# Attention scores from three products of high and low halves, with eight probability buffers, in a fused hybrid decoder block

## The chip, the cores and the metric

One program runs on one core of a Trainium2 chip. The metric is the device time of one execution in microseconds (us); lower is better. Engines are named as in the profile: PE is TensorE (PEld its weight loads), DVE is VectorE, ACT is ScalarE, POOL is GpSimd, SP is SyncE. A name with a q behind it (ACTq, POOLq) is that engine's sequencer, which issues DMAs.

## What is computed

One decoder block over 512 tokens of width 2048, all in float32. The part that the change touches is the sliding-window attention: 16 query heads of 64 dimensions on 2 key/value heads, in blocks of 128 queries that each see 256 keys (the first block only its own 128).

```python
def sliding_window_gqa_sinks(q, k, v, sinks):
    ...
    s = jnp.einsum('bnqhgd,bnkhd->bnhgqk', qb, kb).astype(jnp.float32) / math.sqrt(HEAD_DIM)
    ...
    s = jnp.where(mask[None, :, None, None], s, jnp.finfo(jnp.float32).min)
    p = jax.nn.softmax(jnp.concatenate([s, sink], axis=-1), axis=-1)[..., :-1]
    o = jnp.einsum('bnhgqk,bnkhd->bnqhgd', p.astype(v.dtype), vb)

def reference(x, ...):
    h = rms_norm(x, norm_mix_pre)
    z = h @ w_in                      # q | k | v | u | two gates
    q, k = partial_rope(q, pos), partial_rope(k, pos)
    o_attn = sliding_window_gqa_sinks(q, k, v, sinks)
    o_ssm = s5_mixer(u, ...)          # diagonal complex state space model, GELU, GLU
    mixed = (g_attn * (o_attn @ w_branch[:Q_W]) + g_ssm * (o_ssm @ w_branch[Q_W:])) @ w_out
    x = x + rms_norm(mixed, norm_mix_post)
    a = jax.nn.relu(rms_norm(x, norm_mlp_pre) @ w_up)
    return x + rms_norm((a * a) @ w_down, norm_mlp_post)
```

## The kernel before, in words

**Large products.** Every weight matrix is streamed in 436 units of 128x1024 elements through a ring of four. SP loads a unit (L333), ACT rounds it to the fp32r type as the high half `w_hi` (`hi`, L514), DVE subtracts to get the low half `w_lo` (`lo`, L908), and PE multiplies it with the high and low halves of the activations in three fp32r products, high by high, low by high and high by low (`product`, L1641 to L1643), 24 matmuls a unit. ACT may convert unit n once PE has finished unit n-4 (`unit_done`). PE waits for `lo_ready` at each unit. I call the stretch in which PE works on unit n "slot n"; the program of each engine is written as a loop over n, and n on ACT and DVE runs some slots ahead of PE.

**What else lies in the slots.** Units 0 to 15 give q, 16 to 19 give k and v, 20 to 35 the state space input u, 36 to 99 the gates. Small work is put by hand between the conversions. On DVE at n = 9 to 19, `normed` reads a PSUM bank pair of q and `rope_q` rotates it; at n = 8 to 22 the parameters of the state space model are worked out (`params_at`: `coefficients`, `powers`, `b_bar`, `b_even`, `b_lo`). The coefficients leave through a small round trip: PE turns them, ACT copies them at n = 16 (L620, `rows_ready`), POOL stores them (L366) and loads them back spread over the channels (L371, eight DMAs, `coef_landed`), and DVE's `b_bar` at n = 20 waits for them. ACT stores the resulting weights at n = 23 (L613, 2 MB, `b_stored`), and `load_bw(0)` at n = 26 brings back the first part with eight DMAs issued on ACT's queue (L567), after DVE has cleared the buffer (`clear_bw`, L1154, at n = 24). PE first needs that buffer in slot 37 (`bu`, L1749), a product in four row groups of 32.

**The attention.** It runs in eight groups of eight heads (4 pairs), two groups for each block of 128 queries. In slot 24 + g PE computes the scores of group g, in slot 25 + g ACT and DVE do exponentials and the normalisation, in slot 26 + g PE transposes the probabilities, and in slot 27 + g it multiplies them with v. Each of these is cut in four parts k = 0 to 3, put between the four quarters of a unit on PE:

```python
for b in range(2):
    r = slice(HEAD * b, HEAD * b + HEAD)
    ins = mm(side[:, b, first_key(g):2 * P], Q[r, a % 8, n * P:n * P + P],
             KTOK[r, n * P - P + first_key(g):n * P + P], start=True, stop=True)
ins.then_inc(scores_done, 1)
```

So one part a = 4g + k computes two heads, one on partitions 0 to 63 and one on 64 to 127, plain float32 operands, with 256 columns, or 128 in groups 0 and 1 (`first_key`). I call these 24 long and 8 short parts. The waits around them: PE's scores of part a wait until DVE has read the part before (`scores_read`); DVE's `mask_scores(a)` (L1117) waits for `scores_done` and, since the probability buffer `PB` is used in turn, for the transposes of part a - `NPB` (`trans_done`); PE's transposes (L1709) wait for `probs_ready` and for ACT's copy of the transposes before (L580, `pt_ready`). On DVE a slot is: mask of part 0, `lo` of unit n (and in some slots `normed` of u), mask 1, `maxima`, mask 2, `normalise` of the group before, mask 3, `maxima`. On ACT it is: copy (L580) and four exponentials (L588) for k = 0 and 1, copies for k = 2 and 3, the copy of the output (L595), then `hi` of the next unit.

**POOL** loads constants at the start (L359 to L363: the rotary tables, the identity, the mask and `b_rows`), does the round trip above, then waits for `bl_ready`, builds `rotation(0)` (13 us of small operations) and scales the first weights (`c_by_a`, `b_by_state`). `rotation(0)` is first read by DVE in slot 37.

Of the kernel before, what the change touches and what calls it, by code (L numbers as in the profile page):

```python
# [30 lines left out]
P = 128  # L31
# [61 lines left out]
def build(nc, wstream, xT, x_rows, gains, gain_rows, params, b_rows, b_state, c_pad, consts, cols, out):  # L93
# [26 lines left out]
    U = at("u", [CT, T], 112)  # L120
    Q = at("q", [8, T], 128)
    MH = at("m_hi", [KT, T], 112, F32R)

    NPB = 12
    PB = at("probs", [NPB, 2, 256], 144)
# [4 lines left out]
    KTOK = at("k_t", [T], 176)  # L130
    VTOK = at("v_tok", [TT_N, P], 178.5)
    MASK = at("mask", [2 * P], 181)
    SUM0 = at("square_sum", [4, T], 183)
    BB = at("b_bar", [CT, 2, SSM_S], 191)
    BE = at("b_even", [CT, 2, SSM_S], 195)
    tmp = [at(f"param{k}", [4 * ST if k in (8, 9) else ST], 144 + 0.5 * k) for k in range(11)]
    CT4 = at("coef_rows", [P], 150)
    CW = at("coef_by_channel", [4, NW], 160)
    BC = at("b_parts", [CT, 2, 2, 2, SSM_S], 144, F32R)
    BT = [at(f"b_bar_tmp{k}", [CT, SSM_S], 112 + 2 * k) for k in range(2)]  # L140

# [62 lines left out]
    with ExitStack() as ctx:  # L204
# [3 lines left out]
        def sem(name):  # L208
# [7 lines left out]
        x_first, x_landed = [sem(f"x_first{k}") for k in range(4)], [sem(f"x_landed{s}") for s in range(4)]  # L216
        cols_landed = sem("cols_landed")
        first_raw, first_hi, first_lo = sem("first_raw"), sem("first_hi"), sem("first_lo")
# [6 lines left out]
        rope_done, vt_done, v_ready = (  # L225
            sem("rope_done"), sem("vt_done"), sem("v_ready"))
        angle_ready, trig_ready, bb_ready, b1_ready = (
            sem("angle_ready"), sem("trig_ready"), sem("bb_ready"), sem("b1_ready"))
# [74 lines left out]
        def first_key(g):  # L303

            return P if g < 2 else 0
# [41 lines left out]
        def _(pool):  # L347
# [12 lines left out]
            pool.dma_start(IDENT[:], consts[:, 1024:1152]).then_inc(consts_landed, 16)  # L360
            pool.dma_start(MASK[:], consts[:, 1152:1408]).then_inc(consts_landed, 16)
            for r in range(2):
# [89 lines left out]

            pool.wait_ge(start_ready, 1)
            plink(nc.gpsimd.memset(CBD[:], 0.0))
            load_c(0)
            load_b(0)
            pool.wait_ge(bl_ready, 2)
            rotation(0)
            c_by_a(0)
            b_by_state(0)  # L460
            pool.wait_ge(o_ready, 8)
            for c in range(1, CT):
# [45 lines left out]
        def _(act):  # L508
# [89 lines left out]
            for n in range(8, U_GATE):  # L598
# [12 lines left out]
                if n == 23:  # L611
                    act.wait_ge(bl_ready, 2)
                    act.dma_start(b_dram.rearrange("p c a e r s -> p (c a e r s)"),  # L613
                                  BC[:].rearrange("p c a e r s -> p (c a e r s)").bitcast(F32)).then_inc(b_stored, 16)
                if n == 26:
                    act.wait_ge(b_stored, 16)
                    load_bw(0)
# [271 lines left out]
        def _(v):  # L889
# [186 lines left out]
            def normed(out_, b):  # L1076

                v.wait_ge(unit_done, UNIT_END[b])
                link_to(tt(out_, pair(b), both(RSTD[:]), ALU.mult), bank_read, b + 1)

            SWAP = [r ^ 8 if r < ROT else r for r in range(32)]

            def rope_q(b):
                x = Q[:, 2 * b:2 * b + 2]
                v.wait_ge(consts_landed, 48)
                link(nc.vector.stream_shuffle(KV[:], x, SWAP))
                tt(x, x, both(ROPE[:, 0]), ALU.mult)
                link(tt(KV[:], KV[:], both(ROPE[:, 1]), ALU.mult))
                link_to(tt(x, x, KV[:], ALU.add), rope_done, b + 1)
# [63 lines left out]
            def clear_bw(k):  # L1153
# [30 lines left out]
                         16: ((rotation_start, 0),), 17: ((rotation_start, 1),),  # L1184
                         20: ((b_bar,),), 21: ((b_even,),), 22: ((b_lo, 0), (b_lo, 1)), 24: ((clear_bw, 0),)}
            def low_and_inputs(n):
# [5 lines left out]
            for n in range(8, U_GATE):  # L1192
# [9 lines left out]
                if n in (11, 12, 15, 19):  # L1202
                    rope_q({11: 0, 12: 1, 15: 2, 19: 3}[n])
                if n == 21:
                    normed(KV[:], 4)
                if n == 23:
                    rope_k()
                if n == N_SLOT0 + 2:
                    v.wait_ge(b_stored, 16)
                if n >= N_SLOT0 + 2:  # L1210
# [412 lines left out]
        def _(pe):  # L1623
# [43 lines left out]
            for n in range(8, U_U):  # L1667
# [4 lines left out]
                if n == 13:  # L1672
                    pe.wait_ge(consts_landed, 48)
                    pe.wait_ge(coef_ready, 1)
                    nc.tensor.transpose(side[:, 2, 0:P], AST[:, 0:4].rearrange("p k s -> p (k s)"), IDENT[:]
                                        ).then_inc(coef_turned, 1)


            def attention(slot, k):
# [13 lines left out]
                for g in group_of(slot, N_SLOT0):  # L1693
                    a, n = 4 * g + k, g // 2
                    if a >= 1:
                        pe.wait_ge(scores_read, a)
                    for b in range(2):
                        r = slice(HEAD * b, HEAD * b + HEAD)
                        ins = mm(side[:, b, first_key(g):2 * P], Q[r, a % 8, n * P:n * P + P],  # L1699
                                 KTOK[r, n * P - P + first_key(g):n * P + P], start=True, stop=True)  # L1700
                    ins.then_inc(scores_done, 1)
# [11 lines left out]
            for n in range(U_U, U_GATE):  # L1713
# [3 lines left out]
                if n == N_SLOT0:  # L1717
                    pe.wait_ge(rope_done, 5)
                    pe.wait_ge(v_ready, 1)
# [387 lines left out]
```

## Time and profile before

| | us |
|---|---|
| median of 3 runs | 2497.89 (2497.19 to 2498.23) |
| the profiled execution's own time | 2496.64 |
| its span in the trace | 2494.8 |
| PE busy | 2480.9 (99%) |
| DVE busy | 1278.3 (51%) |
| ACT busy | 683.5 (27%) |
| POOL busy | 175.3 (7%) |

The span is what lies between the first and the last record of the profile; the time of the execution has 1.8 us more. Busy time counts overlapping matmuls once. TensorE's granted clock is 0.999 of full speed. A float32 matmul leaves two records in the trace (the x4 of a part's scores is two matmuls), an fp32r matmul one. All that the change touches runs in the first 290 us.

### The profile page before, as it was taken

What the parts mean: (1) busy time and instruction counts of PE and PEld (TensorE: products, weight loads), DVE (VectorE), ACT (ScalarE), POOL (GpSimd) and SP (SyncE); (2) the same over time, 40 slices, a digit from 0 to 9 for tenths busy, and PEclk for the clock granted to TensorE, in tenths of its full rate; (3) what the DMA queues carried; (4) which work ended last, traced back from release to release, by engine and by line L of the source; (5) the groups of instructions that cost most, each with busy time, mean ns of one, the idle gap of its engine ahead of it and who ended that gap; (6) DMA issues with size and microseconds to landing.
All of it is one profiled execution on the core that took longest, in us unless ns stands there. A gap on an engine that the chain in (4) does not pass through costs nothing.

```text
span 2494.8 us, 30358 instructions
## 1 busy us (share of the span) xinstructions
PE 2480.9 (99%) x11741; PEld 2026.8 (81%) x11741; DVE 1278.3 (51%) x1621; ACT 683.5 (27%) x906; POOL 175.3 (7%) x283
## 2 busy tenths in 40 slices
PE   9999999999999999999999999999999999999998
PEld 7866887877888888888888888888888888888887
DVE  7876688896434432264444444344444344444436
ACT  5146222333422222252122222212222221222223
POOL 1120344430000000000000000000000000000000
PEclk9999999999999999999999999999999999999999
DMA  6431343443334453343332332233332223333242
GB/s 218 113 114 43 109 132 106 131 123 102 126 95 151 143 181 97 110 161 102 102 102 91 104 100 93 84 101 101 99 100 95 92 85 100 101 101 101 92 160 101
DMA packets 83592, 278.22 MB, mean 112 GB/s; under 512 B 17984, under 2 KB 18048, under 8 KB 81472
## 3 DMA queue, kind: packets, MB, share of 16 engines
q1 hardware_dynamic: 64368, 233.34, 28.9%
q0 software_dynamic: 6480, 26.55, 3.3%
q10 hardware_dynamic: 12672, 17.34, 2.0%
q8 instruction: 50, 0.82, 0.1%
q14 instruction: 22, 0.18, 0.0%
HBM read 258.24 MB, written 18.94 MB: 111 GB/s over the span
## 4 chain that ended last, share of the span: by engine, by line
PE 97%; DVE 2%; DMA 1%; ACT 0%; issue 0%; ACTq 0%; POOL 0%; DVEq 0%
PE main L1641 15%; PE main L1643 15%; PE main L1642 15%; PE side L1837 6%; PE side L1836 6%; PE side L1835 6%; PE main L1836 5%; PE main L1837 5%; PE main L1835 5%; PE side L1642 5%; PE side L1641 5%; PE side L1643 5%; PE side L1699 1%; PE side L1709 1%; PE side L1780 1%; PE side L1688 1%
## 5 line engine op out<-in xcount | busy, mean ns | idle before, releaser
L514 ACT ACTIVATE w_hi<-w_raw 128x1024 fp32r<-128x1024 f32 x435 | 452.6, 1056 | 1079.0 <-PE main L1643 403.3
L908 DVE TENSOR_TENSOR w_lo<-w_raw,w_hi 128x1024 fp32r<-128x1024 f32 x435 | 529.1, 1234 | 358.9 <-ACT w_hi L514 340.0
L1641 PE MATMUL main<-h_hi,w_hi 128*128 128x512 f32 x1280 | 505.7, 395 | 1.3 <-DVE h_lo L924 0.7
L1643 PE MATMUL main<-h_hi,w_lo 128*128 128x512 f32 x1280 | 499.2, 390 | 0.0
L1642 PE MATMUL main<-h_lo,w_hi 128*128 128x512 f32 x1280 | 498.9, 390 | 0.0
L1641 PEld LDWEIGHTS main<-h_hi,w_hi 128*128 128x128 f32 x1280 | 240.6, 188 | 56.8 <-issue 4.7
L1643 PEld LDWEIGHTS main<-h_hi,w_lo 128*128 128x128 f32 x1280 | 240.7, 188 | 50.8
L1642 PEld LDWEIGHTS main<-h_lo,w_hi 128*128 128x128 f32 x1280 | 240.9, 188 | 48.0
L1641 PE MATMUL side<-h_hi,w_hi 128*128 128x512 f32 x512 | 199.2, 389 | 0.0
L1642 PE MATMUL side<-h_lo,w_hi 128*128 128x512 f32 x512 | 199.2, 389 | 0.0
L1643 PE MATMUL side<-h_hi,w_lo 128*128 128x512 f32 x512 | 199.2, 389 | 0.0
L1835 PE MATMUL main<-w_hi,a_hi 128*128 128x512 f32 x496 | 192.9, 389 | 0.0
L1836 PE MATMUL main<-w_hi,a_lo 128*128 128x512 f32 x496 | 192.9, 389 | 0.0
L1837 PE MATMUL main<-w_lo,a_hi 128*128 128x512 f32 x496 | 192.9, 389 | 0.0
L1835 PE MATMUL side<-w_hi,a_hi 128*128 128x512 f32 x496 | 192.9, 389 | 0.0
L1836 PE MATMUL side<-w_hi,a_lo 128*128 128x512 f32 x496 | 192.9, 389 | 0.0
L1837 PE MATMUL side<-w_lo,a_hi 128*128 128x512 f32 x496 | 192.9, 389 | 0.0
L1513 DVE TENSOR_TENSOR mlp_acc<-side,mlp_acc 128x1024 f32<-128x1024 f32 x60 | 70.7, 1220 | 151.3 <-PE side L1837 151.3
L1513 DVE TENSOR_TENSOR mlp_acc<-main,mlp_acc 128x1024 f32<-128x1024 f32 x58 | 68.3, 1220 | 151.2 <-PE main L1837 151.2
L834 ACT ACTIVATE a_hi<-a 128x1024 fp32r<-128x1024 f32 x31 | 32.9, 1061 | 377.3 <-DVE a L1498 377.3
L1641 PEld LDWEIGHTS side<-h_hi,w_hi 128*128 128x128 f32 x512 | 96.1, 188 | 20.0
L1643 PEld LDWEIGHTS side<-h_hi,w_lo 128*128 128x128 f32 x512 | 96.1, 188 | 19.9
(332 smaller groups left out, 3131.2 us busy)
## 6 DMA issues: line engine op xcount, KB each, us to landing
w_raw<-wstream SPq DMA_DIRECT2D x435, 512.0 KB, 3.5
gate_scratch<-gate_stage ACTq DMA_DIRECT2D x16, 512.0 KB, 3.9
gate_attn<-gate_scratch POOLq DMA_DIRECT2D x8, 512.0 KB, 3.7
gate_ssm<-gate_scratch POOLq DMA_DIRECT2D x8, 512.0 KB, 4.4
x_rows<-x_rows POOLq DMA_DIRECT2D x4, 1024.0 KB, 11.6
x_scratch<-x_rows ACTq DMA_DIRECT2D x4, 1024.0 KB, 4.0
x_all<-x_scratch POOLq DMA_DIRECT2D x4, 1024.0 KB, 8.1
x<-x_t POOLq DMA_DIRECT2D x6, 512.0 KB, 6.6
```

The lines of the kernel that those rows point to most:

```text
L514: nc.scalar.activation(WH[:, s], RAW[:, s], ACT.Copy).then_inc(hi_ready, 1)
L834: nc.scalar.activation(AH[:, buf, 2 * half:2 * half + 2], AA[:], ACT.Copy).then_inc(ah_ready, 1)
L908: tt(WL[:, s], RAW[:, s], WH[:, s].bitcast(F32), ALU.subtract).then_inc(lo_ready, 1)
L1513: ins = tt(o, ps, o, ALU.add)
L1641: mm(o, wh, xh[:, k0 + k], start=first and k == 0, stop=False)
L1642: mm(o, wh, xl[:, k0 + k], start=False, stop=False)
L1643: ins = mm(o, wl, xh[:, k0 + k], start=False, stop=last and k == 3)
L1688: ins = mm(side[HEAD * b:HEAD * b + HEAD, 3], VTOK[:, n + kb - 1, HEAD * b:HEAD * b + HEAD], PTB[:, b, kb].rearrange("p a q -> p (a q)"), ...
L1699: ins = mm(side[:, b, first_key(g):2 * P], Q[r, a % 8, n * P:n * P + P], KTOK[r, n * P - P + first_key(g):n * P + P], start=True, stop=True)
L1835: mm(banks[:, t], xh[:, k0 + k, r], wh[:, c], start=first and k == 0, stop=False)
L1836: mm(banks[:, t], xl[:, k0 + k, r], wh[:, c], start=False, stop=False)
L1837: ins = mm(banks[:, t], xh[:, k0 + k, r], wl[:, c], start=False, stop=last and k == 1)
```

## The change

It splits q and k after the rotary step into high halves (`QH` in two tiles, `KH`; ACT copies to fp32r) and low halves (`QL`, `KL`; DVE subtractions), and PE forms each part's scores as three fp32r products, high by high, low by high and high by low, accumulated in the same PSUM banks. To make room for these tiles, `NPB` goes from 12 to 8, the `b_rows` input and its products move to where x lay (so that their load waits on POOL for the end of the reading of x), the mask is loaded later, `rotation(0)` waits for the last scores, and `clear_bw(0)` and `load_bw(0)` move from n = 24 and 26 to n = 34 and 35.

```diff
...
     Q = at("q", [8, T], 128)
+    QL = at("q_lo", [8, T], 128, F32R)
+    QH = [at(f"q_hi{k}", [4, T], kib, F32R) for k, kib in enumerate((191, 160))]
+    KH = at("k_hi", [T], 180, F32R)
+    KL = at("k_lo", [T], 176, F32R)
     MH = at("m_hi", [KT, T], 112, F32R)
...
-    NPB = 12
+    NPB = 8
     PB = at("probs", [NPB, 2, 256], 144)
...
     KTOK = at("k_t", [T], 176)
-    VTOK = at("v_tok", [TT_N, P], 178.5)
-    MASK = at("mask", [2 * P], 181)
+    VTOK = at("v_tok", [TT_N, P], 178)
+    MASK = at("mask", [2 * P], 182)
     SUM0 = at("square_sum", [4, T], 183)
-    BB = at("b_bar", [CT, 2, SSM_S], 191)
-    BE = at("b_even", [CT, 2, SSM_S], 195)
+    BB = at("b_bar", [CT, 2, SSM_S], 112)
+    BE = at("b_even", [CT, 2, SSM_S], 116)
...
-    CW = at("coef_by_channel", [4, NW], 160)
+    CW = at("coef_by_channel", [4, NW], 176)
...
-    BT = [at(f"b_bar_tmp{k}", [CT, SSM_S], 112 + 2 * k) for k in range(2)]
+    BT = [at(f"b_bar_tmp{k}", [CT, SSM_S], 120 + 2 * k) for k in range(2)]
...
-        cols_landed = sem("cols_landed")
+        cols_landed, mask_landed = sem("cols_landed"), sem("mask_landed")
         first_raw, first_hi, first_lo = sem("first_raw"), sem("first_hi"), sem("first_lo")
...
             sem("rope_done"), sem("vt_done"), sem("v_ready"))
+        qkh_ready, qkl_ready = sem("qkh_ready"), sem("qkl_ready")
...
             pool.dma_start(IDENT[:], consts[:, 1024:1152]).then_inc(consts_landed, 16)
-            pool.dma_start(MASK[:], consts[:, 1152:1408]).then_inc(consts_landed, 16)
+            pool.wait_ge(xsq_ready, 4)
+            pool.wait_ge(xl_ready, KT)
             for r in range(2):
...
             pool.wait_ge(start_ready, 1)
+            pool.wait_ge(bl_ready, 2)
+            pool.dma_start(MASK[:], consts[:, 1152:1408]).then_inc(mask_landed, 16)
             plink(nc.gpsimd.memset(CBD[:], 0.0))
...
             load_b(0)
-            pool.wait_ge(bl_ready, 2)
-            rotation(0)
             c_by_a(0)
             b_by_state(0)
+            pool.wait_ge(scores_done, 32)
+            rotation(0)
             pool.wait_ge(o_ready, 8)
...
                                   BC[:].rearrange("p c a e r s -> p (c a e r s)").bitcast(F32)).then_inc(b_stored, 16)
-                if n == 26:
+                if n in (12, 13, 16, 20):
+                    b = (12, 13, 16, 20).index(n)
+                    act.wait_ge(rope_done, b + 1)
+                    t = 2 * b % 4
+                    nc.scalar.activation(QH[b // 2][:, t:t + 2], Q[:, 2 * b:2 * b + 2], ACT.Copy).then_inc(qkh_ready, 1)
+                if n == 24:
+                    act.wait_ge(rope_done, 5)
+                    nc.scalar.activation(KH[:], KTOK[:], ACT.Copy).then_inc(qkh_ready, 1)
+                if n == 35:
                     act.wait_ge(b_stored, 16)
...
+            def q_lo(b):
+                v.wait_ge(qkh_ready, b + 1)
+                t = 2 * b % 4
+                x = slice(2 * b, 2 * b + 2)
+                link_to(tt(QL[:, x], Q[:, x], QH[b // 2][:, t:t + 2].bitcast(F32), ALU.subtract), qkl_ready, b + 1)
+
+            def k_lo():
+                v.wait_ge(qkh_ready, 5)
+                link_to(tt(KL[:], KTOK[:], KH[:].bitcast(F32), ALU.subtract), qkl_ready, 5)
+
             SWAP = [r ^ 8 if r < ROT else r for r in range(32)]
...
                 x = Q[:, 2 * b:2 * b + 2]
-                v.wait_ge(consts_landed, 48)
+                v.wait_ge(consts_landed, 32)
                 link(nc.vector.stream_shuffle(KV[:], x, SWAP))
...
                          16: ((rotation_start, 0),), 17: ((rotation_start, 1),),
-                         20: ((b_bar,),), 21: ((b_even,),), 22: ((b_lo, 0), (b_lo, 1)), 24: ((clear_bw, 0),)}
+                         20: ((b_bar,),), 21: ((b_even,),), 22: ((b_lo, 0), (b_lo, 1)), 24: ((k_lo,),), 34: ((clear_bw, 0),)}
             def low_and_inputs(n):
...
                     rope_q({11: 0, 12: 1, 15: 2, 19: 3}[n])
+                if n in (13, 14, 17, 21):
+                    q_lo((13, 14, 17, 21).index(n))
                 if n == 21:
...
                 if n == N_SLOT0 + 2:
+                    v.wait_ge(mask_landed, 16)
                     v.wait_ge(b_stored, 16)
...
                 if n == 13:
-                    pe.wait_ge(consts_landed, 48)
+                    pe.wait_ge(consts_landed, 32)
                     pe.wait_ge(coef_ready, 1)
...
                         pe.wait_ge(scores_read, a)
-                    for b in range(2):
-                        r = slice(HEAD * b, HEAD * b + HEAD)
-                        ins = mm(side[:, b, first_key(g):2 * P], Q[r, a % 8, n * P:n * P + P],
-                                 KTOK[r, n * P - P + first_key(g):n * P + P], start=True, stop=True)
+                    qh, ql = QH[a % 8 // 4][:, a % 4], QL[:, a % 8]
+                    for i, (q, key) in enumerate(((qh, KH), (ql, KH), (qh, KL))):
+                        for b in range(2):
+                            r = slice(HEAD * b, HEAD * b + HEAD)
+                            ins = mm(side[:, b, first_key(g):2 * P], q[r, n * P:n * P + P],
+                                     key[r, n * P - P + first_key(g):n * P + P], start=i == 0, stop=i == 2)
                     ins.then_inc(scores_done, 1)
...
                 if n == N_SLOT0:
-                    pe.wait_ge(rope_done, 5)
+                    pe.wait_ge(qkl_ready, 5)
                     pe.wait_ge(v_ready, 1)
...
                         (lambda k: attention(n, k)) if n >= N_SLOT0 else None)
...
```

The change moves instructions at three places on which terms of the prediction rest. The rows give, per engine, the program's order: line, instruction, tile written and tiles read, shape, and the semaphores waited for. `q_hi_63` and `q_hi_64` are the two tiles of `QH`.

PE, a long part in slot 26, before (one row stands for two heads; behind the scores lie the transposes):

```order
L1643 MATMUL main<-h_hi,w_lo 128x512
L1699 MATMUL side<-k_t,q 128x256 [waits scores_read]
L1699 MATMUL side<-k_t,q 128x256
L1709 MATMUL side<-ident,probs 128x128 [waits pt_ready,probs_ready]
L1709 MATMUL side<-ident,probs 128x128
```

and now:

```order
L1672 MATMUL main<-h_hi,w_lo 128x512
L1730 MATMUL side<-k_hi,q_hi_63 128x256 [waits scores_read]
L1730 MATMUL side<-k_hi,q_hi_63 128x256
L1730 MATMUL side<-k_hi,q_lo 128x256 x2
L1730 MATMUL side<-k_lo,q_hi_63 128x256 x2
L1740 MATMUL side<-ident,probs 128x128 [waits pt_ready,probs_ready]
L1740 MATMUL side<-ident,probs 128x128
```

Two float32 matmuls have become six fp32r ones; the waits before and behind them are the same.

ACT, from the end of n = 34 to n = 36, before (the `load_bw(0)` DMAs stood ten conversions earlier):

```order
L580 ACTIVATE probs_t<-side 128x4x128 [waits pv_done,trans_done] x2
L595 ACTIVATE q<-side 128x4x128 [waits pv_done]
L514 ACTIVATE w_hi<-w_raw 128x1024 [waits unit_done,raw_landed3]
L580 ACTIVATE probs_t<-side 128x4x128 [waits pv_done,trans_done] x4
L595 ACTIVATE q<-side 128x4x128 [waits pv_done]
```

and now:

```order
L588 ACTIVATE probs_t<-side 128x4x128 [waits pv_done,trans_done] x2
L603 ACTIVATE q<-side 128x4x128 [waits pv_done]
L522 ACTIVATE w_hi<-w_raw 128x1024 [waits unit_done,raw_landed3]
L575 DMA b_weights_111<-b_scratch 16x8x64 [waits bw_zeroed,b_stored]
L575 DMA b_weights_111<-b_scratch 16x8x64 x7
L588 ACTIVATE probs_t<-side 128x4x128 [waits pv_done,trans_done] x4
L603 ACTIVATE q<-side 128x4x128 [waits pv_done]
```

The eight DMA issues now stand between the conversion of unit 35 and the four copies of the last group's transposes, which PE waits for in slot 33.

ACT around n = 16, where it copies the turned coefficients, before:

```order
L514 ACTIVATE w_hi<-w_raw 128x1024 [waits unit_done,raw_landed0]
L620 ACTIVATE coef_rows<-side 128x128 [waits coef_turned]
L514 ACTIVATE w_hi<-w_raw 128x1024 [waits unit_done,raw_landed1]
```

and now:

```order
L522 ACTIVATE w_hi<-w_raw 128x1024 [waits unit_done,raw_landed0]
L627 ACTIVATE q_hi_64<-q 128x1024 [waits rope_done]
L636 ACTIVATE coef_rows<-side 128x128 [waits coef_turned]
L522 ACTIVATE w_hi<-w_raw 128x1024 [waits unit_done,raw_landed1]
```

The copy of the coefficients now stands behind the high half of the third pair of q, which waits for DVE's rotary step.

## Rows read from the trace of the kernel before

**Rows 1.** The page: busy time, and the chain that ended last by engine.
```profile
PE 2480.9 (99%) x11741; PEld 2026.8 (81%) x11741; DVE 1278.3 (51%) x1621; ACT 683.5 (27%) x906; POOL 175.3 (7%) x283
...
PE 97%; DVE 2%; DMA 1%; ACT 0%; issue 0%; ACTq 0%; POOL 0%; DVEq 0%
```
**Rows 2.** PE's waits in the first 600 us: us in total, times, longest.
```profile
PE side L1709 <- ACT probs_t L580: 0.5, 1, 0.5
PE main L1641 <- DVE w_lo L908: 0.5, 1, 0.5
```
**Rows 3.** Timeline of PE, a long part, slot 30 (start us, us, what).
```profile
192.75 0.70 PE L1699 MATMUL side<-k_t,q 64*128 64x256 f32 x4
193.38 0.66 PE L1709 MATMUL side<-ident,probs 128*128 128x128 f32 x4
193.79 0.47 PE L1641 MATMUL main<-h_hi,w_hi 128*128 128x512 f32 x1
```
**Rows 4.** Timeline of PE, a short part, slot 24.
```profile
143.18 0.49 PE L1699 MATMUL side<-k_t,q 64*128 64x128 f32 x4
143.60 0.50 PE L1641 MATMUL main<-h_hi,w_hi 128*128 128x512 f32 x1
```
**Rows 5.** Timeline of PE, an fp32r product in four row groups.
```profile
269.83 1.70 PE L1749 MATMUL side<-u_hi_lo,b_weights 32*128 32x256 f32 x48
271.46 0.50 PE L1641 MATMUL main<-h_hi,w_hi 128*128 128x512 f32 x1
```
**Rows 6.** Timeline of ACT at n = 26 in the kernel before.
```profile
136.66 3.98 ACTq L567 DMA_DIRECT2D b_weights<-b_scratch  x8
```
**Rows 7.** Timelines of ACT, DVE and PE in slots 32 and 33.
```profile
235.98 2.19 DVE L1108 TENSOR_SCALAR probs<-probs,softmax_sum 128x256 f32<-128x256 f32 x8
237.69 1.06 ACT L514 ACTIVATE w_hi<-w_raw 128x1024 fp32r<-128x1024 f32 x1
240.56 0.60 ACT L580 ACTIVATE probs_t<-side 128x512 f32<-128x512 f32 x1 [1.81 <-PE side L1709]
241.75 0.60 PE L1709 MATMUL side<-ident,probs 128*128 128x128 f32 x4
```
**Rows 8.** Timeline of DVE around the clearing of the first weight buffer.
```profile
135.66 0.91 DVE L1154 MEMSET b_weights<- 128x1024 f32 x1 [0.16 <-issue]
```
**Rows 9.** Timelines of DVE and PE in slot 30.
```profile
193.55 0.69 DVE L1117 SCALAR_TENSOR_TENSOR probs<-side,mask 128x512 f32<-128x512 f32 x1 [1.38 <-issue]
...
195.35 0.70 PE L1699 MATMUL side<-k_t,q 64*128 64x256 f32 x4
...
202.03 0.69 DVE L1117 SCALAR_TENSOR_TENSOR probs<-side,mask 128x512 f32<-128x512 f32 x1
```
**Rows 10.** Timelines of DVE and PE at unit 14 (`lo` on DVE, first matmul on PE).
```profile
81.03 1.23 DVE L908 TENSOR_TENSOR w_lo<-w_raw,w_hi 128x1024 fp32r<-128x1024 f32 x1
86.72 0.47 PE L1641 MATMUL main<-h_hi,w_hi 128*128 128x512 f32 x1
```
**Rows 11.** The coefficients' round trip: ACT, DVE (end of the third rotary step), the tile's DMAs.
```profile
87.00 0.28 ACT L620 ACTIVATE coef_rows<-side 128x128 f32<-128x128 f32 x1 [4.10 <-PE side L1675]
89.70 1.23 DVE L1089 TENSOR_TENSOR q<-q,kv_raw 128x1024 f32<-128x1024 f32 x1
L371 POOL DMA_DIRECT2D coef_by_channel<-coef_scratch x8: 628/636/648, 90.3 to 94.7; - x8
DMA to landing us min/median/max: 4.6/9.6/12.4
109.37 0.69 DVE L1021 TENSOR_TENSOR b_bar_tmp<-b_bar,coef_by_channel 128x512 f32<-128x512 f32 x1
```
**Rows 12.** Timelines of DVE and PE at unit 22.
```profile
119.68 1.22 DVE L1079 TENSOR_TENSOR kv_raw<-main,rstd 128x1024 f32<-128x1024 f32 x1 [4.86 <-PE main L1643]
124.80 1.22 DVE L908 TENSOR_TENSOR w_lo<-w_raw,w_hi 128x1024 fp32r<-128x1024 f32 x1
130.72 0.47 PE L1641 MATMUL main<-h_hi,w_hi 128*128 128x512 f32 x1
```

## The prediction

> **What bounds the kernel now.** I read the page first. PE is busy 99% of the span, and the chain that ended last lies 97% on PE [rows 1]. Then the waits of PE: in the first 600 us, where the whole change lies, it waits for another engine hardly ever, 0.5 us once for a low half and 0.5 us once, in slot 32, for ACT's copy of a transpose [rows 2]. So PE's own stream is the kernel's time. A change can move it in two ways only: by what the altered matmuls take between their neighbours, and by a new wait on PE. Work added to DVE and ACT is free as long as it stays ahead of PE. Last I read the timelines at the touched places, for starts rather than durations: the durations of overlapping matmuls add up to more than the time that passes, while the start of the next group minus the start of this one is what a group costs.
>
> **The long parts (24).** A part starts at 192.75 and the transposes behind it at 193.38: 0.63 us for two heads of 256 columns [rows 3]. A short part takes 143.60 - 143.18 = 0.42 us [rows 4]. The difference, 0.21 us for 128 more columns, leaves 0.42 - 0.21 = 0.21 us that does not depend on the columns (the first weight load, laid open, and the change back). If a float32 product is four passes at one column per cycle of 2.4 GHz, 128 columns take 4 x 0.053 = 0.21 us, just this difference, and both heads run side by side in their row groups: nothing is left for a second head.
>
> The new parts are three fp32r products for each head. Their nearest row is the product in four row groups of 32, also fp32r, also 256 columns: 48 matmuls, that is 12 rounds of four at a time, take 271.46 - 269.83 = 1.63 us [rows 5]. Less the same 0.21 us this is 0.118 us a round. Three rounds then take 0.21 + 3 x 0.118 = 0.56 us; with the bare 0.107 us of 256 columns, 0.53 us. I take 0.55 us, since the last round has no load behind it that it must wait for. Saving 0.08 us x 24 = **1.9 us** (bounds 1.7 and 2.4).
>
> **The short parts (8).** No fp32r matmul of 128 columns is in the trace. From below, three rounds at 0.053 us give 0.21 + 0.16 = 0.37 us; from above, if a round costs as much as with 256 columns, 0.56 us. The nearest row is four transposes of 128 columns, 193.79 - 193.38 = 0.41 us, 0.10 us apiece, twice what their columns need [rows 3]: another thing than the columns paces them, and the next weight load is the likely one. I take 0.21 + 2 x 0.11 + 0.053 = 0.48 us, 0.06 to 0.07 us more than now, x 8 = **+0.5 us** (bounds -0.4 and +1.1).
>
> The Trainium skill (FP8 and Floating Point Precision, TensorE Precision Notes) says that true float32 takes four passes through the array; three in place of four would by that alone save 24 x 0.107 + 8 x 0.053 = 3.0 us. The Trainium skill also says (TensorE: Matmul & The Clock Gate, LDWEIGHTS) that a weight load takes the number of its columns divided by 1.2 GHz, an estimate of 107 ns for 128 columns whatever the rows. By that page a short product is held by its load, and the change makes the short parts slower; the trace agrees with it in the 0.10 us of a transpose.
>
> **The moved DMA issue.** `load_bw(0)` costs ACT's queue 3.98 us for its eight DMAs [rows 6]. At n = 26 nobody waited for ACT. Now it stands at n = 35, between `hi` of unit 35 and the first copy of the last group's transposes. `hi` begins at 237.69; the DMAs also wait for DVE's `clear_bw`, which now comes after the last `normalise`, ended at 238.17 [rows 7], and takes 0.91 us [rows 8]: 239.1. The issues end at 243.1. The copy of part 0 stood at 240.56, as soon as the transposes were there; now it runs from 243.1 to 243.7. PE needs it before the transposes of part 1, which stood at 241.75 [rows 7]. So PE waits **1.9 us** in slot 33. After that ACT has caught up: the copies of parts 1 to 3 take 0.6 us in a quarter of 1.8 us. Bounds: 0 if the issues do not hold the copy up, 4 us if all of them fall on PE. The buffer lands some 3 us later, long before slot 37 at 269.83 [rows 5].
>
> **Eight buffers in place of twelve.** DVE's mask of part a now waits for the transposes of part a - 8, which PE does in the same quarter right behind the scores. Mask 0 of slot 30 started at 193.55; it would now start when the transposes have ended, at 193.79 plus the 0.17 us that lay between 193.38 and 193.55: about 193.95. It ends at 194.65, and PE wants `scores_read` for the next scores at 195.35 [rows 9]: 0.7 us of room, also in parts 1 and 2. In the slots with `normed` of u (28 is one) `lo` and `normed`, 1.2 us each, stand between masks 0 and 1; there mask 1 starts at 4.3 us after the first scores and ends at 5.0, and the third scores come at 5.05: no room, no wait. Mask 3 stands behind `normalise` at 202.03 and moves by 0.4 us; the next scores come 3 us later. I cost this at nothing. The cover is that 0.7 us; what comes without it is a rival.
>
> **Halves of q and k, and the coefficients.** DVE gets four subtractions of 1.23 us (the row of `lo` [rows 10]) and one of half that, ACT four copies of 1.06 us and one of 0.6. Neither is waited for while DVE's `lo` ends well before PE's unit starts. At unit 14 it ends at 82.26 against 86.72, 4.5 us of room [rows 10]; one subtraction stands before it (part 0, at n = 13), so 3.2 us stay, and the same at unit 16 after two. The longest detour is the coefficients. ACT copied them at 87.00; now the third high half stands before, which waits for the rotary step that ended at 90.93 [rows 11] and comes 2.5 us later by the two new subtractions, at 93.4; with its own 1.06 us the copy starts at 94.5, 7.5 us late. The eight loads were issued from 90.3 to 94.7 and take up to 12.4 us; the last would land at 107.1 plus 7.5 = 114.6, while DVE comes to `b_bar` at 109.37 + 2 [rows 11]. DVE then waits 3 us. Behind it stand `lo` of unit 21 (which PE comes to only 5 us after `normed` has begun), the last `q_lo`, and `normed` of k and v, which waited 4.9 us for PE anyway [rows 12] and takes up the most of it. About 1.5 us reach `lo` of unit 22: it ended at 126.0 against PE's 130.72 [rows 12], so 3 us of room stay. Cost nothing.
>
> **The rest.** The mask is issued on POOL at about 130; with the longest landing of the coefficients' loads, 12.4 us [rows 11], it is there before the first scores end at 143.6 [rows 4]. `rotation(0)` takes 13 us from the last scores on, which end before 236 [rows 7], and is needed behind the product at 270 [rows 5]. The 0.6 MB that leave POOL's queue at the start lay behind all of x, so x lands no sooner. Nothing for each.
>
> **Sum.** -1.9 + 0.5 + 1.9 = +0.5 us. The profiled execution took 2496.64 us (span 2494.8), so 2497.1 for its like; the median of the runs is 1.25 us above it, which gives **2498.4 us**. A measurement of this kernel can tell about 0.2%, 5 us, from no change: this is no change.
>
> **The rivals.**
> - *The issue does not stall* (DVE or the queue is quicker): -1.4 us, 2496.5. For it speaks that a part of the 3.98 us overlaps `hi`; against, that 2 us of it would have to vanish. 0.12.
> - *Passes alone count*, loads are hidden: the parts save 3.0 us in place of 1.4, net -1.1 us, 2496.8. The 0.10 us of a transpose speaks against it. 0.05.
> - *Short fp32r products run at float32's speed*, 0.21 us a round: 0.21 + 3 x 0.21 = 0.84 us, 0.35 us more than taken, x 8 = +2.8, net +3.3 us, 2501.2. Nothing of 128 columns in fp32r excludes it. 0.12.
> - *The coefficients come later still* than DVE can absorb: past 3 us more, PE waits in slot 22; with 5 us more, +2, net +2.5 us, 2500.9. 0.05.
> - *The buffers run short* (the other side): where DVE reaches a mask over 0.7 us after the transposes, PE waits for `scores_read`. At most the whole shift of 0.4 us would fall on each long part, 9.6 us; at 0.3 us each 24 x 0.3 = +7.2, net +7.7 us, 2506.1. For it: in two slots of eight there is no room behind mask 1, by the sum above. 0.08.
> - *The change does not do what it says*: the two heads do not run side by side in the six matmuls. Six rounds are 0.21 + 6 x 0.118 = 0.92 us, +0.29 us in each long part, +7.0, and about 0.35 x 8 = +2.8 in the short ones less what was counted: net some +12 us, 2510. The float32 parts and the four row groups speak against it. 0.03.
>
> **How the numbers follow.** The forecast has 0.53. Slower by over 0.2%: the buffers and the heads, 0.11. Faster by over 0.2%: no case reaches it, since the 32 parts together last 24 x 0.63 + 8 x 0.42 = 18.5 us and a third of that would have to go; 0.02 for what I do not see. The same: 0.53 + 0.12 + 0.05 + 0.12 + 0.05 = 0.87. The range runs from below the first two rivals (2496.5, less 0.7 for the scatter of the runs) to above the third (2501.2 plus 1.3); it leaves out 0.13.
>
> **What would show it.** In the profile after: a long part 0.55 us from its start to the transposes' start, a short one 0.48; one wait of PE of 1.9 us in slot 33, put down to ACT's copy of the transposes; the coefficient copy near 94.5 and DVE idle 3 us before `b_bar`; masks 0 to 2 of a slot 0.4 us later behind the scores, and no wait of PE for DVE's mask. I am wrong if PE waits for masks, if a short part takes over 0.6 us, or if slot 33 shows no wait.

## The result, and the profile after

The changed kernel takes 2500.46 us (median of 22 runs, 2498.23 to 2502.25) against 2496.43 us (22 runs, 2495.0 to 2499.18) for the kernel before on the same chips: a ratio of 1.0013, interval 1.0007 to 1.0019, which is +3.2 us (1.7 to 4.7); the two medians themselves lie 4.0 us apart. The difference is inside the 0.2% that the prediction called no change, and inside its range, but the interval excludes the +0.5 us of its sum. Ratios, here and below, are taken over fast runs alone: three far slower executions, 3012 us of the kernel before and 7477 and 8840 us in experiments 7 and 8, are left out of them. The profiled execution took 2498.86 us with a span of 2496.7.

The page of the changed kernel, busy time:

```profile
PE 2479.8 (99%) x11805; PEld 2030.8 (81%) x11805; DVE 1285.5 (51%) x1626; ACT 687.3 (28%) x911; POOL 172.8 (7%) x283
```

PE is as full as before [rows 1]. Its waits in the first 600 us (us in total, times, longest):

```profile
PE side L1740 <- ACT probs_t L588: 2.9, 2, 2.4
PE main L1670 <- DVE h_lo L940: 1.8, 2, 1.1
PE side L1686 <- POOL ones L353: 1.1, 1, 1.1
```

The first row answers to the first of [rows 2]: 0.5 us of it is the old wait in slot 32, 2.4 us is new. No row names DVE's mask. The timeline of PE, a short part and what follows it, then a long part (start us, us, what). The long part lies in slot 29, as does that of [rows 3]; the heading there says 30, but PE starts unit 29 at 189.32 and unit 30 at 201.61 in the kernel before:

```profile
142.52 0.33 PE L1730 MATMUL side<-k_hi,q_hi 64*128 64x128 f32 x2
142.68 0.28 PE L1730 MATMUL side<-k_hi,q_lo 64*128 64x128 f32 x2
142.80 0.28 PE L1730 MATMUL side<-k_lo,q_hi 64*128 64x128 f32 x2
143.00 0.50 PE L1670 MATMUL main<-h_hi,w_hi 128*128 128x512 f32 x1
...
191.57 0.38 PE L1730 MATMUL side<-k_hi,q_hi 64*128 64x256 f32 x2
191.79 0.28 PE L1730 MATMUL side<-k_hi,q_lo 64*128 64x256 f32 x2
191.91 0.28 PE L1730 MATMUL side<-k_lo,q_hi 64*128 64x256 f32 x2
192.12 0.66 PE L1740 MATMUL side<-ident,probs 128*128 128x128 f32 x4
```

A short part takes 143.00 - 142.52 = 0.48 us, a long one 192.12 - 191.57 = 0.55 us, against 0.42 [rows 4] and 0.63 us [rows 3]. These are the two values that the prediction took.

The timelines of ACT, DVE and PE in slot 33:

```profile
235.44 1.06 ACT L522 ACTIVATE w_hi<-w_raw 128x1024 fp32r<-128x1024 f32 x1
236.46 0.91 DVE L1180 MEMSET b_weights<- 128x1024 f32 x1 [0.28 <-DVE probs L1134]
237.45 3.73 ACTq L575 DMA_DIRECT2D b_weights<-b_scratch  x8
241.29 0.60 ACT L588 ACTIVATE probs_t<-side 128x512 f32<-128x512 f32 x1 [4.79 <-issue]
242.03 0.63 PE L1740 MATMUL side<-ident,probs 128*128 128x128 f32 x4 [2.37 <-ACT probs_t L588]
```

The chain is the one foretold, each link a little later: the clearing ends at 237.37, the eight issues at 241.2, the copy goes at once, and PE resumes after 2.37 us.

**Where the time went.** I compare the start of PE's units between two traces, counted from unit 8 on, so that what differs at the start of an execution drops out. The changed kernel is 0.43 us later at unit 26 (eight short parts, 0.054 us each), 1.58 us earlier at unit 32 (24 long parts, -2.01 us in all, 0.084 each), 1.59 us earlier at unit 33, and 0.97 us later at unit 34: 2.56 us are lost in slot 33. From there to unit 140 the difference does not move. Then a second thing comes, far from the change. PE's granted clock in four stretches of the changed kernel (columns: busy time and instructions of PE, its weight loads, DVE, ACT, POOL, then the granted clock):

```profile
1085.00:1090.00 5.00, 4.31 (x36) 4.11 (x35) 4.93 (x8) 4.97 (x10) 0.00 (x0) 1.00 0.50 201
1090.00:1094.80 4.80, 2.98 (x25) 2.77 (x25) 4.73 (x9) 3.19 (x4) 0.00 (x0) 1.00 0.57 191
1094.80:1098.20 3.40, 3.40 (x19) 3.40 (x17) 1.43 (x2) 0.00 (x0) 0.00 (x0) 0.50 0.76 192
1098.20:1103.00 4.80, 4.80 (x43) 4.80 (x43) 1.66 (x4) 1.90 (x5) 0.00 (x0) 1.00 0.22 86
```

Behind a stretch in which PE had idled 1.8 of 4.8 us the clock stands at its lower level, 1.2 in place of 2.4 GHz, and PE is 1.5 us later behind it than in the execution shown of before, in which the clock stayed up. PE idles there in both kernels, for a low half of the weights (`w_lo`) that stands behind DVE's row work between the two halves of the block (PE's waits from 600 us on):

```profile
PE main L1934 <- DVE w_lo L924: 2.5, 2, 1.8
```

That such a fall can come without the change, and stay away with it, is seen in the experiments: such a fall is there in the traces of five of them, one of which is the kernel before with a single number altered (the sixth below), and absent in the three others, all of which contain the change.

### The profile page after: what moved, and what is told of

Same layout as the page of the kernel before. It is cut to its first block, busy times and chain, and to the rows that moved or that the text cites. A ratio compares the mean times of both kernels' runs of the same rounds, so it can differ in the third digit from the quotient of the medians.

```text
span 2496.7 us, 30503 instructions
## 1 busy us (share of the span) xinstructions
PE 2479.8 (99%) x11805; PEld 2030.8 (81%) x11805; DVE 1285.5 (51%) x1626; ACT 687.3 (28%) x911; POOL 172.8 (7%) x283
## 4 chain that ended last, share of the span: by engine, by line
PE 97%; DVE 1%; ACT 0%; DMA 0%; ACTq 0%; issue 0%; DVEq 0%
PE main L1670 15%; PE main L1672 15%; PE main L1671 15%; PE side L1866 6%; PE side L1868 6%; PE side L1867 6%; PE main L1866 5%; PE main L1868 5%; PE main L1867 5%; PE side L1672 5%; PE side L1671 5%; PE side L1670 5%; PE side L1730 1%; PE side L1811 1%; PE side L1740 1%; PE side L1780 1%
## 5 line engine op out<-in xcount | busy, mean ns | idle before, releaser
L1671 PEld LDWEIGHTS side<-h_lo,w_hi 128*128 128x128 f32 x512 | 96.1, 188 | 19.9
```

The source lines that it names most:

```text
L1671: mm(o, wh, xl[:, k0 + k], start=False, stop=False)
```

## The experiments

Theory A: the fp32r parts save 1.6 us, and the new wait of PE in slot 33 costs more than that, by itself and by falls of the clock that it brings. Theory B: the part that the trace does not show lies in the moved loads, the new tiles and the halves.

**1. The load after the attention.**

```diff
-                if n == 35:
-                    act.wait_ge(b_stored, 16)
-                    load_bw(0)
...
                 if n == U_GATE:
                     attention(n - 2)
+                    act.wait_ge(b_stored, 16)
+                    load_bw(0)
                     act.wait_ge(bank_read, 6)
```

> The changed kernel with the eight DMAs of load_bw(0) issued at n = 36, behind the last attention work of ACT, in place of n = 35. Theory A (the wait in slot 33 is what makes the change slower): PE's 2.4 us of new wait in slot 33 goes, the transposes of part 1 come at most 0.4 us behind the low product before them; against the kernel before the time falls to 1.4 us below it (parts -1.6), ratio 0.9994, and if the wait also brought falls of the clock, the mean granted clock is back at that of the kernel before. Theory B (what the trace of the changed kernel does not show, some 2 us between its own sum of +1.0 and the measured +3.2, comes from the moved loads and the new tiles): only 2.4 us go, ratio 1.0003 or more.

Measured: 2495.43 us, ratio 0.9997 (0.9988 to 1.0006), 5 us below the changed kernel's median. Slot 33 costs nothing more: PE's units stand 1.60 us before those of the kernel before from unit 33 to unit 140. Of 11 runs none has a mean clock of 0.997, seven have 0.999. PE's waits for ACT's copy are back at 0.5 us:

```profile
PE side L1739 <- ACT probs_t L588: 0.5, 1, 0.5
```

Between the changed kernel and this one lie 4.0 us by the ratios and 5.0 by the medians, more than the 2.4 us of the wait, as A has it and B not. The intervals are too wide for this run to settle it alone: 1.0003, B's value, lies within this one. Nor does the ratio tell this kernel from the kernel before.

**2. The kernel before with the late load.**

```diff
-                if n == 26:
+                if n == 35:
                     act.wait_ge(b_stored, 16)
                     load_bw(0)
...
-                         20: ((b_bar,),), 21: ((b_even,),), 22: ((b_lo, 0), (b_lo, 1)), 24: ((clear_bw, 0),)}
+                         20: ((b_bar,),), 21: ((b_even,),), 22: ((b_lo, 0), (b_lo, 1)), 34: ((clear_bw, 0),)}
```

> The kernel before with clear_bw(0) and load_bw(0) moved to n = 34 and 35, nothing else. Theory A: one new wait of PE of 2.4 us in slot 33, put down to ACT's copy of the transposes; ratio 1.0010, up to 1.0016 if the wait also brings falls of the clock. Theory B: ratio 1.0010 at most, clock unchanged.

Measured: 2500.68 us, ratio 1.0016 (1.0007 to 1.0025). With nothing of the scores, halves and buffers changed, this one move makes the kernel as slow as the whole change does. Slot 33 costs 4.87 us in its trace, of which 3.1 us is the wait (the issues took 4.70 us here). The rest is the clock:

```profile
239.00:244.60 5.60, 2.52 (x16) 1.90 (x15) 0.47 (x1) 0.68 (x2) 0.00 (x0) 1.00 0.52 141
244.60:248.00 3.40, 3.40 (x12) 2.72 (x11) 0.00 (x0) 0.83 (x2) 0.00 (x0) 0.51 0.00 0
248.00:251.00 3.00, 3.00 (x16) 2.24 (x14) 0.00 (x0) 1.52 (x4) 0.00 (x0) 0.99 0.01 3
```

PE is busy 2.5 of the 5.6 us in which the wait lies, and the stretch behind runs at half clock. Six of 11 runs have a mean clock of 0.997, none of the 27 runs of the kernel before beside them. (Beside experiments 5 to 8, on another chip, three of its 28 runs have it.)

**3. Float32 scores in the changed kernel.** `q_lo` and `k_lo` alone are multiplied.

```diff
-                    for i, (q, key) in enumerate(((qh, KH), (ql, KH), (qh, KL))):
-                        for b in range(2):
-                            ...
+                    for b in range(2):
+                        r = slice(HEAD * b, HEAD * b + HEAD)
+                        ins = mm(side[:, b, first_key(g):2 * P], QL[r, a % 8, n * P:n * P + P].bitcast(F32),
+                                 KL[r, n * P - P + first_key(g):n * P + P].bitcast(F32), start=True, stop=True)
```

> The changed kernel with its scores as two plain float32 products per part, as before the change; they read the low halves alone, so that the scores leave out the high halves. Everything else stays. Both theories: a long part takes 0.63 us again and a short one 0.42 us, so PE has 24 x 0.085 - 8 x 0.055 = +1.6 us more than the changed kernel; slot 33's wait stays at 2.4 us. Against the kernel before +4.7 us by the measured +3.2, ratio 1.0019; if it comes out at 1.0013 the fp32r parts bring nothing in the whole kernel.

Measured: 2501.8 us, ratio 1.0021 (1.0012 to 1.003). Up to unit 33 its PE units stand within 0.01 us of those of the kernel before. So the halves, the eight buffers, the later coefficients and the moved POOL work cost PE nothing there, and the 1.6 us is the scores' alone. Slot 33 costs 4.1 us, again with a stretch at half clock behind it:

```profile
241.40:245.40 4.00, 1.67 (x10) 1.25 (x9) 0.00 (x0) 1.19 (x2) 0.00 (x0) 1.00 0.67 182
245.40:248.80 3.40, 3.40 (x11) 2.73 (x10) 0.00 (x0) 0.60 (x1) 0.00 (x0) 0.50 0.00 0
```

That is 2.3 us of wait and some 1.8 us more, against 0.2 us more in the changed kernel's own trace, where no fall followed. The fall is worth 1.6 us.

**4. The products done twice.**

```diff
-                    for i, (q, key) in enumerate(((qh, KH), (ql, KH), (qh, KL))):
+                    for i, (q, key) in enumerate(((qh, KH), (ql, KH), (qh, KL), (qh, KH), (ql, KH), (qh, KL))):
...
-                                     key[r, n * P - P + first_key(g):n * P + P], start=i == 0, stop=i == 2)
+                                     key[r, n * P - P + first_key(g):n * P + P], start=i == 0, stop=i == 5)
```

> The changed kernel with the three products of each part done twice into the same sum (scores doubled). It prices a further round of two fp32r products in two row groups: with 256 columns 0.115 us, so a long part takes 0.55 + 3 x 0.115 = 0.90 us; with 128 columns 0.11 us if the weight load paces it (short part 0.48 + 0.33 = 0.81 us), 0.055 us if the columns do (0.65 us).

Measured (one run, 2510.06 us), PE's timeline of a short part:

```profile
142.43 0.33 PE L1730 MATMUL side<-k_hi,q_hi 64*128 64x128 f32 x2
142.59 0.28 PE L1730 MATMUL side<-k_hi,q_lo 64*128 64x128 f32 x2
142.71 0.28 PE L1730 MATMUL side<-k_lo,q_hi 64*128 64x128 f32 x2
142.82 0.28 PE L1730 MATMUL side<-k_hi,q_hi 64*128 64x128 f32 x2
142.93 0.27 PE L1730 MATMUL side<-k_hi,q_lo 64*128 64x128 f32 x2
143.04 0.28 PE L1730 MATMUL side<-k_lo,q_hi 64*128 64x128 f32 x2
143.25 0.50 PE L1670 MATMUL main<-h_hi,w_hi 128*128 128x512 f32 x1
```

It is 0.11 us from round to round with 128 columns. Unit 26 comes 2.53 us later than in the changed kernel, that is 2.53 / 24 = 0.105 us for each further round, and units 26 to 32 take 8.6 us more, 8.6 / 72 = 0.119 us with 256 columns. Half the columns save only about a tenth of the time: something that does not shrink with them paces a short round. That two heads run side by side follows too: single fp32r matmuls of 256 columns over all 128 rows start 0.12 us apart (at 1091.25 and 1091.37 in the changed kernel's trace), and a round of two takes no longer. Slot 33 has a wait of 2.5 us here as well, and no fall of the clock behind it.

**5. Half of the load at n = 35, the other half at n = 36.**

```diff
-            def load_bw(c):
+            def load_bw(c, quarters=range(4)):
...
-                for q in range(4):
+                for q in quarters:
...
-                    load_bw(0)
+                    load_bw(0, (0, 1))
...
+                    load_bw(0, (2, 3))
                     act.wait_ge(bank_read, 6)
```

> The changed kernel with only four of the eight DMAs of load_bw(0) at n = 35 and four at n = 36. Theory A (the length of ACT's issue, from the end of DVE's clearing on, sets PE's wait in slot 33): the issue ends 1.85 us sooner, the wait falls from 2.4 us to about 0.5 us, and no fall of the clock follows in slot 33; parts -1.6 and wait +0.5 against the kernel before, with 0.4 us outside the span: ratio 0.9998. A rival, that any DMA issue there costs the whole wait: 2.4 us stay, ratio 1.0010 or more.

Measured: 2495.84 us, ratio 0.9994 (0.9985 to 1.0002); slot 33 costs 0.62 us in place of 2.56. Four issues of 1.78 us end at 239.4, and the copy follows:

```profile
237.61 1.78 ACTq L575 DMA_DIRECT2D b_weights<-b_scratch  x4
239.49 0.60 ACT L588 ACTIVATE probs_t<-side 128x512 f32<-128x512 f32 x1 [2.85 <-issue]
```

The loss goes down by 1.94 us, as much as the issues are shorter (3.73 - 1.78 = 1.95), and the interval leaves out the rival's 1.0010. One run of 11 has a mean clock of 0.997.

**6. Eight buffers in the kernel before** (`NPB = 12` becomes `NPB = 8`, nothing else; one execution).

> The kernel before with eight probability buffers in place of twelve, nothing else. If the buffers cost nothing (as predicted): DVE's masks 0 to 2 start some 0.4 us later behind the scores, put down to the transposes, but a slot of PE keeps its 12.3 us and slots 24 to 33 their sum to 0.1 us. If they run short: PE waits for DVE's mask, some 0.1 to 0.3 us in each long part, 2 to 7 us in all.

Measured: one run, 2497.87 us. PE's units stand within 0.01 us of those of the kernel before from unit 8 to unit 140. DVE's waits between 143 and 256 us:

```profile
DVE probs L1117 <- PE side L1709: 12.3, 17, 1.4
DVE w_lo L908 <- ACT w_hi L514: 10.3, 3, 8.0
DVE probs L1117 <- PE side L1699: 5.1, 7, 1.5
```

In 17 of its masks DVE now waits for the transposes (L1709) in place of the scores, and PE notices nothing. The clock fell behind the idle stretch near 1094 us here too, and once near the start, at 8.6 us; the mean clock of this execution is 0.997, with no wait in slot 33.

**7. The coefficients first, with the load at n = 36.** On top of experiment 1:

```diff
-                if n in (12, 13, 16, 20):
-                    b = (12, 13, 16, 20).index(n)
-                    ...
...
                 if n == 16:
                     act.wait_ge(coef_turned, 1)
                     nc.scalar.activation(CT4[:], side[:, 2, 0:P], ACT.Copy).then_inc(rows_ready, 1)
+                if n in (12, 13, 16, 20):
+                    b = (12, 13, 16, 20).index(n)
+                    ...
```

> The changed kernel with load_bw(0) at n = 36 (as in the first experiment) and at n = 16 the copy of the turned coefficients ahead of the high half of q. If the later coefficients cost PE nothing (as predicted): DVE's wait of 4.5 us before b_bar shrinks below 1 us, the room of unit 22 goes from 1.8 us back to 4 us or more, and the time stays that of the first experiment, 2495.4 us, ratio 0.9997. If it costs something hidden: 0.9993 or less.

Measured: 2495.75 us, ratio 0.9995 (0.9986 to 1.0004). DVE no longer waits for the coefficients at all, and PE's units are where they were in experiment 1. The detour was hidden.

**8. The clearing one slot earlier** (`clear_bw` at n = 33 in place of 34, the DMAs still at n = 35).

> The changed kernel with clear_bw(0) at n = 33, before DVE's last normalise, and the eight DMAs still at n = 35. Theory A: the issue no longer waits for DVE, starts 0.1 us after the conversion of unit 35, some 1.9 us sooner, and PE's wait in slot 33 falls from 2.4 to 0.5 us, ratio 0.9998. If the issue's own 3.7 us decide whatever the start: 2.4 us stay, ratio 1.0010 or more.

Measured: 2495.43 us, ratio 0.9993 (0.9984 to 1.0002), which leaves out 1.0010; slot 33 costs nothing. The timeline of ACT:

```profile
235.10 0.34 ACTq L575 DMA_DIRECT2D b_weights<-b_scratch  x1
...
235.92 1.06 ACT L522 ACTIVATE w_hi<-w_raw 128x1024 fp32r<-128x1024 f32 x1
235.95 2.86 ACTq L575 DMA_DIRECT2D b_weights<-b_scratch  x6
238.91 0.60 ACT L588 ACTIVATE probs_t<-side 128x512 f32<-128x512 f32 x1 [1.93 <-PE side L1740]
```

I had expected the issues to begin behind the conversion and 0.5 us of wait to stay. They begin before it: the first starts at 235.10, ahead even of the start of the conversion (235.92) that stands before it in the program. ACT's queue here hands out DMAs while the activations ahead of them are still to be done, so most of the 3.7 us lies beside the output copy and the conversion once the clearing is no longer waited for.

## Why the prediction was right, and where it was off

**What bounds the kernel**: right. Everything that was added to DVE, ACT and POOL was free, and the one wait that reached PE cost its full length.

**The long and the short parts**: right to 0.01 us a part, -2.01 and +0.43 us against -1.9 and +0.5. Experiment 4 bears out the step from which the short parts' loss followed, a pace of 0.105 us a round set by something other than the columns. With it the rival in which passes alone count falls, and the one of short products at float32's speed, and that of heads which do not run side by side. That it is the weight load was not tried by itself. By the Trainium skill (TensorE: Matmul & The Clock Gate, LDWEIGHTS) a weight load takes its columns divided by 1.2 GHz, an estimate of 107 ns for 128 columns; the measured 105 ns agrees with it.

**The moved DMA issue**: the mechanism was right, the size was too small, and this is the step that put the sum off. I had 1.9 us; the wait was 2.37 us in the profiled execution, and 2.3, 2.5 and 3.1 us in experiments 3, 4 and 2. The last `normalise` ended 0.3 us later as PE sees it (it came 1.99 us sooner than in the trace before, PE's unit 33 2.25 us sooner), the clearing began 0.3 us after it, where I had let it follow at once, the first issue came another 0.1 us behind the clearing's end, the copy 0.1 us behind the last issue, and PE resumed 0.15 us behind the copy; the issues themselves were 0.25 us shorter than in [rows 6]. The sum also lacked what follows such a wait. Behind the wait of experiments 2 and 3 the clock fell to 1.2 GHz, which cost 1.6 us each time; behind that of experiment 4 and of the changed kernel's own trace it did not. For the other executions there is only the mean clock, which does not say where a fall lay: of the changed kernel's 22 runs ten have 0.997, and they average 2500.9 us against 2499.4 for the twelve others. I had read TensorE's clock as a constant 0.999 and looked for no wait that might touch it.

**The accounts**: -1.6 for the parts, +2.6 in slot 33, and +0.4 us by which every kernel that contains the change takes longer outside its span (2498.86 - 2496.7 = 2.2 us against 1.8): +1.4 us without falls of the clock. If half of the executions have a fall behind the wait, an estimate from two of four traces and ten of 22 mean clocks, 0.5 x 1.6 = +0.8 comes on top. That gives +2.2 us, within the measured 1.7 to 4.7, but 1.0 us under its middle. The spans point to more falls than that: the trace of the changed kernel has one fall, near 1095 us, and a span of 2496.7 us, and the median span of its 22 runs is 2498.25 us, about one fall longer. Where these falls lie, and whether the change brings them all, is not shown; nor is where the 0.4 us comes from.

**Eight buffers**: right, cost nothing (experiment 6), though DVE's masks did wait for the transposes as said. The room was smaller than I had it. In slot 29 of the changed kernel:

```profile
192.91 0.69 DVE L1143 SCALAR_TENSOR_TENSOR probs<-side,mask 128x512 f32<-128x512 f32 x1 [1.23 <-PE side L1740]
...
194.09 0.39 PE L1730 MATMUL side<-k_hi,q_hi 64*128 64x256 f32 x2
```

The mask ends at 193.60, 0.5 us before the next scores, where I had 0.7; it starts 1.34 us behind its own scores (191.57), 0.5 us later than before, where I had 0.4.

**The coefficients**: right in that it cost nothing (experiment 7), too rosy in the room:

```profile
DVE b_bar_tmp L1037 <- DMA coef_by_channel<-coef_scratch: 4.5, 1, 4.5
...
127.02 1.23 DVE L924 TENSOR_TENSOR w_lo<-w_raw,w_hi 128x1024 fp32r<-128x1024 f32 x1
...
130.06 0.47 PE L1670 MATMUL main<-h_hi,w_hi 128*128 128x512 f32 x1
```

DVE waited 4.5 us before `b_bar` in place of 3, and `lo` of unit 22 ended at 128.25, 1.8 us before PE came, not 3.

**Two of the rivals' times** were added up 0.5 us too high: +2.5 us on 2497.9 is 2500.4, not 2500.9, and +7.7 is 2505.6, not 2506.1. Neither moves the range or a chance.

**No gain to speak of**: with the load out of the way the change is worth its 1.6 us on PE less the 0.4 us outside, a ratio of 0.9995. The three kernels that do this (experiments 1, 7 and 8) have ratios of 0.9993 to 0.9997, 4 to 5 us below the changed kernel, but each interval against the kernel before holds 1, as does that of experiment 5. No version was found that is faster beyond the measurement.

## What to carry to other kernels

When a buffer's new place makes a load move, ask what stands behind its issue on the queue of the engine that issues it: eight small DMAs held ACT for 3.7 us, and one slot made the difference between free and 2.6 us, more than the change could earn. Where TensorE is full, price a matmul by the distance of starts in rows of its kind, with the round's pace and the cost of entering and leaving apart; here three fp32r products beat one float32 product with 256 columns (0.55 us against 0.63 for two heads) and lost with 128 (0.48 against 0.42). A stall of TensorE can cost more than its length, for the clock may fall behind it: 1.6 us on top of waits of 2.3 and 3.1 us.

## What the runs showed of the hardware that was not expected

- Four traces have a wait of 2.3 to 3.1 us in slot 33. Right behind it the granted clock fell to 0.5 in two of them (experiments 2 and 3) and not in the two others (the changed kernel and experiment 4); in the six traces without that wait it stayed up there. One fall cost 1.6 us. The mean clocks of the other executions point the same way: 10 of 22, 6 of 11 and 7 of 11 runs have 0.997 in the changed kernel and experiments 2 and 3, and two of 43 where the wait is 0.6 us or less (experiments 1, 5, 7 and 8). But a mean clock does not say where a fall lay, nor does it count them well: experiment 6 has 0.997 with falls at 8.6 and 1094 us, and experiment 3 has 0.998 with falls at 245 and 1099 us.
- A fall of the same size can come near 1095 us, behind a stretch that the change leaves alone: in the trace of the changed kernel and in those of experiments 1, 2, 3, 4 and 6, not in those of the kernel before and of experiments 5, 7 and 8. It makes single profiled executions of one kernel differ by 1.5 us. All four traces with the wait in slot 33 have it, and two of the six without; ten traces are too few to say whether the one has to do with the other.
- ACT's queue issued DMAs ahead of activations that stand before them in its program (experiment 8). One issue took 0.34 to 0.59 us: eight took 3.73 us in the changed kernel, 3.98 in the kernel before and 4.70 in experiment 2.
